# Sample tokens taken out of the dense expert stages of a PEER decoder step and served by fetched rows

## The reference, cut to what matters

```python
q = (x @ w_q).reshape(T, 8, 256)
s1, s2 = q[..., :128] @ keys1.T, q[..., 128:] @ keys2.T
v1, i1 = top_k(s1, 16);  v2, i2 = top_k(s2, 16)
sc, pos = top_k(all sums v1 + v2, 16)          # 128 experts per token
idx, gate = i1 * 128 + i2 at pos, softmax(sc)
act = gelu(einsum('tkd,td->tk', u_tab[idx], x)) * gate
out = einsum('tk,tkd->td', act, v_tab[idx])
x = x + out
```

## Time and profile before

| | us |
|---|---|
| median of 3 runs | 2356.89 (2355.27 to 2357.67) |
| profiled execution | 2357.76, span 2356.0 |
| PE busy | 2158.3 (92%) |
| DVE busy | 1722.0 (73%) |
| ACT busy | 1263.2 (54%) |
| POOL busy | 579.2 (25%) |

### The profile page before, as it was taken

The page is one execution under the profiler, slowest core; times in us unless marked ns, Lnnn a source line. Parts: engine busy times, 40 slices in busy tenths (PEclk is TensorE's granted clock), DMA queues, the critical chain, the costliest instruction groups (busy, mean ns, idle before and its releaser), DMA issues.

```text
span 2356.0 us, 53148 instructions
## 1 busy us (share of the span) xinstructions
PE 2158.3 (92%) x18562; PEld 1732.3 (74%) x18562; DVE 1722.0 (73%) x3454; ACT 1263.2 (54%) x2428; POOL 579.2 (25%) x451
## 2 busy tenths in 40 slices
PE   2477989989999999999988898998999999999998
PEld 1355867767888788888866655776788887888886
DVE  8899569966999855555544545999499996555555
ACT  2321468854444455555578454886444444555554
POOL 3996047941000000000037401786200000000000
PEclk7698799999999999999999857999999999999999
DMA  2000334545554455656554204465554545556653
GB/s 79 5 0 1 109 112 146 175 136 164 157 156 152 146 178 177 176 177 180 175 202 147 77 7 155 127 179 158 153 153 151 160 153 156 176 178 176 178 177 117
DMA packets 88953, 328.94 MB, mean 140 GB/s; under 512 B 10785, under 2 KB 10785, under 8 KB 88481
## 3 DMA queue, kind: packets, MB, share of 16 engines
q1 hardware_dynamic: 88272, 318.36, 44.7%
q0 software_dynamic: 592, 9.47, 1.0%
HBM read 321.60 MB, written 6.19 MB: 139 GB/s over the span
## 4 chain that ended last, share of the span: by engine, by line
PE 40%; issue 32%; DVE 21%; POOL 5%; ACT 1%; DVEq 0%; DMA 0%; SPq 0%; POOLq 0%; ACTq 0%
PE ps L282 11%; PE ps L284 11%; PE ps L283 11%; POOL wsp L232 2%; DVE big L800 2%; PE ps L1311 1%; DVE big L789 1%; PE ps L1867 1%; DVE big L1121 1%; DVE big L1130 1%; DVE big L1124 1%; PE ps L888 1%; DVE big L1117 1%; DVE big L1127 1%; DVE big L1149 1%
## 5 line engine op out<-in xcount | busy, mean ns | idle before, releaser
L221 ACT ACTIVATE wsp<-ring 128x512 f16<-128x512 f32 x1200 | 752.5, 629 | 802.0 <-PE ps L284 791.0
L282 PE MATMUL ps<-hs,wsp 128*128 128x288 f16 x2752 | 799.3, 290 | 48.4 <-DVE hs L307 17.6
L283 PE MATMUL ps<-hs,wsp 128*128 128x288 f16 x2752 | 799.2, 290 | 0.0
L284 PE MATMUL ps<-hs,wsp 128*128 128x288 f16 x2752 | 798.6, 290 | 0.0
L234 DVE SCALAR_TENSOR_TENSOR wsp<-ring,wsp 128x512 f16<-128x512 f32 x648 | 446.6, 692 | 406.5 <-ACT wsp L221 406.2
L283 PE MATMUL ps<-hT,wsp 128*128 128x288 f16 (+2 forms) x2560 | 641.0, 263 | 0.0
L282 PE MATMUL ps<-hT,wsp 128*128 128x288 f16 (+2 forms) x2560 | 619.7, 263 | 6.7 <-DVE hT L1451 6.7
L284 PE MATMUL ps<-hT,wsp 128*128 128x288 f16 (+2 forms) x2560 | 619.2, 263 | 0.0
L232 POOL TENSOR_TENSOR wsp<-ring,wsp 128x512 f16<-128x512 f32 x272 | 350.0, 1311 | 187.3 <-ACT wsp L221 186.5
L282 PEld LDWEIGHTS ps<-hs,wsp 128*128 128x128 f16 x2752 | 272.3, 99 | 135.7 <-DVE hs L307 25.4
L284 PEld LDWEIGHTS ps<-hs,wsp 128*128 128x128 f16 x2752 | 273.3, 99 | 73.0
(11 more groups left out here) (251 smaller groups left out, 2167.2 us busy)
## 6 DMA issues: line engine op xcount, KB each, us to landing
ring<-in_v SPq DMA_DIRECT2D x256, 512.0 KB, 3.6
ring<-in_ub SPq DMA_DIRECT2D x184, 512.0 KB, 3.7
ring<-in_ua SPq DMA_DIRECT2D x72, 512.0 KB, 3.7
ring<-in_wq SPq DMA_DIRECT2D x32, 512.0 KB, 3.6
ring<-in_win SPq DMA_DIRECT2D x32, 512.0 KB, 3.8
ring<-in_glu SPq DMA_DIRECT2D x16, 512.0 KB, 3.7
big<-in_hgs POOLq DMA_DIRECT2D x1, 4096.0 KB, 13.6
ring<-in_wout SPq DMA_DIRECT2D x8, 512.0 KB, 4.3
```

The costliest lines, as they stand in the source:

```text
L221: nc.scalar.activation(wsp[:, k % 2, 0, cols], ring[:, k, cols], ACT.Copy, scale=scale).then_inc(hi_ready, 1)
L282: nc.tensor.matmul(out, w_hi, hi, start=start, stop=False, **kw)
L283: nc.tensor.matmul(out, w_hi, lo, start=False, stop=False, **kw)
L284: return nc.tensor.matmul(out, w_lo, hi, start=False, stop=stop, **kw)
```

## The change

The 32 sample tokens leave the dense products of U and V: these have 256 columns now (`TP`), 32 groups of 8 tokens instead of 36, and no cut chunks in V (two chunks share a bank). For the samples each layer fetches the chosen rows instead. 4 copies of the 32 samples fill 128 partitions, each with 2 of the 8 heads, so 32 experts per partition (`SLOTS`). GpSimd fetches one row per partition with an indirect DMA (128 rows of 4 KB, 512 KB), 32 times from a plain copy of U and 32 times from V, into three buffers. VectorE dots each U row with the token (`dot_dve`, one per three blocks of the U loop), ScalarE takes the gelu, and VectorE sums the weighted V rows (`sum_dve`, one per 3.5 blocks of V). Eight small matmuls add the four copies up ahead of V's last four blocks.

With it the stages shift: `ua` has 28 blocks instead of 36, the transposes stand after 24 blocks instead of 40, 4 blocks of `ub` precede the loop, and the loop has 8 bodies of 12 blocks with a group after every third block. ScalarE takes the exponentials after block 20. The selection's third pass has 2 heads on 128 partitions instead of 8 on 32, and runs first; the samples' score lists shrink from 16 to 4. Three fetches stand on GpSimd's queue between its last splits and the fill. The query stage gets eight transposes that lay the samples out by rows. The loops of VectorE over U's bodies and V's blocks are unrolled.

```diff
-UA, UB = 36, 60
+UA = 28
+QH = PH // 4
+SLOTS = QH * TK
+BUFS = 3
...
-        G0 = 5
+        G0 = 1
-        TRIPS, PER = 3, 6
+        TRIPS, PER = 3, 4
-        SPOTS = [0, 2, 4, 6, 8, 10]
+        SPOTS = [0, 3, 6, 9]
+        FETCH = [2, 5, 8, 11]
...
+        def fetch_pool(g, L, a, b):
+            if a == 0:
+                g.wait_ge(pix, 2 * L + 2)
+                g.wait_ge(pxc, L + 1)
+                states_out(g, L)
+            for n in range(a, b):
+                if n >= BUFS:
+                    g.wait_ge(taken, 2 * SLOTS * L + n - BUFS + 1)
+                table, idx = (t_in[f"rows{L}"], row_u) if n < SLOTS else \
+                    (t_in[f"v{L}"].rearrange("j i d -> (j i) d"), row_v)
+                nc.gpsimd.indirect_dma_start(rows[n % BUFS], None, table, bass.IndirectOffsetOnAxis(
+                    ap=idx[:, n % SLOTS:n % SLOTS + 1], axis=0)).then_inc(fetched[n % BUFS], 16)
+        def dot_dve(v, L, n):
+            row_here(v, L, n)
+            r = rows[n % BUFS]
+            nc.vector.tensor_tensor_reduce(r, r, xrep, 1.0, 0.0, ALU.mult, ALU.add,
+                                           zs[:, n:n + 1]).then_inc(taken, 1)
+        def sum_dve(v, L, n):
+            row_here(v, L, SLOTS + n)
+            r, w = rows[(SLOTS + n) % BUFS], ws[:, n:n + 1]
+            v.wait_ge(taken, 2 * SLOTS * L + SLOTS + n)
+            if n == 0:
+                ins = nc.vector.tensor_scalar(acc, r, w, None, ALU.mult)
+            else:
+                ins = nc.vector.scalar_tensor_tensor(out=acc, in0=r, scalar=w, in1=acc, op0=ALU.mult, op1=ALU.add)
+            ins.then_inc(taken, 1)
...
                     if more:
                         weigh(d, q + 1, first)
+                    if kk in FETCH:
+                        dot_dve(v, L, d * len(FETCH) + FETCH.index(kk))
...
-            per_block(pe, f"v{L}", None, post)
+            per_block(pe, f"v{L}", None, post, 0, NK // RING - 1)
+            sample_out_pe(pe, L)
+            per_block(pe, f"v{L}", None, post, NK // RING - 1, NK // RING)
...
             split_pool(g, "ua0")
+            fetch_pool(g, 0, 0, BUFS)
             peer_ones_pool(g, 0)
+            fetch_pool(g, 0, BUFS, 2 * SLOTS)
...
-                peer_u_pe(pe, L, "ua")
-                peer_u_pe(pe, L, "ub", 0, 1)
+                peer_u_pe(pe, L, "ua", 0, 6)
                 peer_tr_pe(pe, L)
-                peer_u_pe(pe, L, "ub", 1, G0)
+                peer_u_pe(pe, L, "ua", 6, 7)
+                peer_u_pe(pe, L, "ub", 0, G0)
...
-                peer_u_act(act, L, "ua")
+                peer_u_act(act, L, "ua", 0, 5)
                 peer_exp_act(act, L)
+                peer_u_act(act, L, "ua", 5, 7)
```

More of the change, by code:

```diff
@@ L109, in build @@
         big = sb("big", [P, NK * T])
+        TAIL = NK * TP
+        xrep = big[:, TAIL:TAIL + D]
+        rows = [big[:, TAIL + D * (1 + k):TAIL + D * (2 + k)] for k in range(BUFS)]
+        sel = sb("sel", [P, TS])
         xT = sb("xT", [P, KC, T])
@@ L319, in x_chunk @@
             else:
-                eng.wait_ge(pacc[k // 2 - 1], sum(len(ACC[m]) for m in range(c + 1)))
+                eng.wait_ge(pacc[k // 2 - 1], c + 2)
         def square(c):
@@ L1031, in build, with turn_x @@
         pah = [sem(f"peer_act_hi{L}") for L in range(2)]
+        pst = sem("peer_scores_sample")
+        pxd = sem("peer_x_spread")
+        pxr = sem("peer_x_turned")
+        pxc = sem("peer_x_copied")
+        pix = sem("peer_rows_known")
+        fetched = [sem(f"peer_rows_fetched{k}") for k in range(BUFS)]
+        taken = sem("peer_rows_taken")
+        pzg = sem("peer_sample_gelu")
+        psw = sem("peer_sample_weights")
+        pso = sem("peer_sample_out")
         pal = [sem(f"peer_act_lo{L}") for L in range(2)]
         def peer_query_pe(pe, L):
+            def turn_x():
+                pe.wait_ge(pxd, L + 1)
+                for c in range(KC):
+                    mm = nc.tensor.transpose(ps[:, 2 + c // 4, (c % 4) * P:(c % 4 + 1) * P],
+                                             rows[0][:, c * P:(c + 1) * P], ident[:, :])
+                mm.then_inc(pxr, 1)
             def scores(i, k, first):
@@ L1053, in after @@
                     scores(i, k - 1, first)
-                elif not first:
+                elif first:
+                    turn_x()
+                else:
                     scores(i - 1, 3, False)
-            project(pe, f"wq{L}", lambda i, k, first: None if first else pe.wait_ge(pq[L], i * 8 + 2 * k - 6), after,
-                    inputs=(1, 4)[L])
+            for trip in range(4):
+                project(pe, f"wq{L}", lambda i, k, first: None if first else pe.wait_ge(pq[L], i * 8 + 2 * k - 6), after,
+                        trip, trip + 1, inputs=(1, 4)[L])
             scores(3, 3, False)
@@ L1086, in post @@
                     scores_out(i - 1, 3)
-            per_block(act, f"wq{L}", split_hi, post, ahead=2, following=[f"ua{L}"] * 2)
+            for trip in range(4):
+                per_block(act, f"wq{L}", split_hi, post, trip, trip + 1, ahead=2, following=[f"ua{L}"] * 2)
             scores_out(3, 3)
@@ L1114, in peer_topk_dve @@
                 v.wait_ge(pss[L], b + 1)
[L1115 to L1131, removed]
+                best([(score[:, b, j * NK:(j + 1) * NK], val[j][:, f, h], idu[j][:, f, h], rest[j][:, :])
+                      for j in range(2)])
+                if h % 4 == 3 and f:
+                    v.wait_ge(pst, 2 * L + h // 4 + 1)
+                    best([(score_s[:, h // 4, n], val[2][:, n, h // 4], idu[2][:, n, h // 4], rest[n][:, :])
+                          for n in range(2)])
         def peer_pairs_dve(v, cnt, L):
@@ L1184, in peer_pairs_dve @@
+                L_(vv.tensor_tensor(paired(ranks(past)), pos2[:, 0:n, None, :].to_broadcast(pair), paired(row(starts)),
                                     ALU.is_ge))
                 cnt.add(vv.tensor_tensor(ranks(picked[0]), ranks(past), row(steps), ALU.mult))
-                L_(vv.tensor_tensor(heads(picked[1]), heads(past), key_steps[0:w, :, None, :].to_broadcast(byhead),
+                L_(vv.tensor_tensor(heads(picked[1]), heads(past), key_steps[:, 0:nh, None, :].to_broadcast(byhead),
@@ L1405, in peer_ug_dve @@
             v.wait_ge(pge[L], GA)
-            g_bodies(v, body, 1)
+            for d in range(BODIES):
+                body(d, d == 0, d == BODIES - 1)
             v.wait_ge(pmul[L], GROUPS)
@@ L1432, in peer_v_act @@
             act.wait_ge(pge[L], NK)
+            sample_gelu_act(act, L)
             def split(act, name, i, k):
```

271 lines of the change are left out of this document (176 added, 95 removed).

## The result

| | before | after |
|---|---|---|
| median, us | 2356.08 (2355.12 to 2357.67, 4 runs) | 2298.09 (2297.08 to 2299.29, 4 runs) |
| ratio | | 0.9753, 95% interval 0.9737 to 0.9770 |
| span of the profiled execution | 2356.0 | 2297.6 |

The account below looks back on a forecast made before the run. TensorE and VectorE were both taken as full in the U loop, TensorE alone in V. Terms: -41 + 17.5 = -23.5 us per layer, -47 for two, from 2357.8 to 2311, range 2258 to 2372.

Parts of the forecast that it names:

- (a): V stage: blocks of 256 instead of 288 columns take 2.62 us instead of 2.95, minus 41 us per layer.
- the cover: V: VectorE's sums should hide behind TensorE's blocks; failing by 0.5 us per sum would cost 16 us per layer.
- a slow start: Start of V: 3 us charged for TensorE's low clock behind a long wait.
- (b): Expert selection before the U loop: a shorter VectorE chain brings TensorE's transposes at 477.5 instead of 518.6, 41 us earlier.
- (c): Transposes to U loop: GpSimd's splits, three fetches and fill precede VectorE's first split, at 512 instead of 572.35 us.
- (d): U loop: a period of 10.04 us; V starts at 834.5 instead of 817.2, plus 17.5 us per layer.
- the round: U loop: circle of VectorE's long iteration, its next split, one TensorE block and ScalarE's high part, 10.04 us per period.
- Rival 1: U loop: VectorE's own work decides, 9.4 us per period, 40 us less than forecast, 2271 us; chance 0.13.
- Rival 2: U loop: only TensorE's columns count, 8.7 us per period, 81 us less than forecast, 2230 us; chance 0.04.
- rival 4: U loop: the dot runs at the scan's rate, period 11.7 us, 102 us more than forecast, 2413; chance 0.06.
- Rival 3: GpSimd: each fetch is slow; 9 us each costs 45 us, all of the gain, 10 gives 2413; chance 0.09.
- Rival 5: U loop and V: two float32 SBUF operands halve the rate of dots and sums, 2.2 us, total 2362; chance 0.06.

Follow-up runs that it names:

- experiment 5: Changed kernel with the weighted sums of fetched v rows over 1 column instead of 1024: 2297.32 us against 2298.09.
- experiment 6: Changed kernel with the transposes behind all 28 first blocks instead of 24, and the exponentials behind 24 instead of 20: 2278.95 us against 2298.09.
- The four runs: Changed kernel with, one at a time: dots over 1 column, 2295.75 us; weighings behind the next split, 2250.40; loop products of 224 columns, 2281.93; dots done twice, 2329.46.
- experiment 2: Changed kernel with the next group's two weighings moved behind the next weight split on VectorE in the U loop: 2250.40 us against 2298.09.
- experiment 3: Changed kernel with TensorE multiplying 224 of the 256 prompt columns in the U loop: 2281.93 us against 2298.09.
- experiment 7: Changed kernel with both full-computation moves, experiment 2 and experiment 6 together: 2231.79 us against 2298.09.

## Why the prediction was right, point by point

The first reciprocal of a norm marks the stages in both traces: before 316.93, 1204.02, 1459.80 and 2347.24; after 318.71, 1175.45, 1429.66 and 2288.82. So the first layer's expert stage gained 30.4 us (23.5 forecast), the second one 28.3, the stage between them 1.6, and the start lost 1.8, which is no effect of the change (in the runs of the experiments, with the same code there, this first reciprocal stood between 316.1 and 318.9).

- **(a) V.** The block of 2.62 us is exact, the cover held (experiment 5), and the transfers came at 258 GB/s against 257, though at a share of 0.78 and not 0.85. From V's start to the next norm's reciprocal it takes 342.95 us; by the prediction, with the 5.9 us from the last product to that reciprocal before, 346. The 3 us charged for a slow start are what is missing: in the first layer TensorE begins V at the 2.4 GHz level, its products 0.11 us apart, with a wait of 3.24 us ahead of it. In the second layer, with the same wait ahead, it begins at the 1.2 GHz level (granted clock 0.50 from 1944.59 to 1947.12, products 0.21 us apart), and V takes 344.23 us, 1.3 more. So the charge was too large in both layers. In the kernel before the low clock had lasted longer (0.51 from 817.16 to 822.83); what decides is open.
- **(b) Selection.** Transposes at 479.10 instead of 477.5, of which 1.8 is the later start. That the sum fits so well is luck, as two errors cancel. The three passes begin, samples first, with these casts:

```profile
396.25 1.11 DVE L1208 CAST big<-big 128x64 f16<-128x64 uint32 x1
...
413.48 1.25 DVE L1208 CAST big<-big 128x256 f16<-128x256 uint32 x1
...
448.20 0.29 DVE L1208 CAST big<-big 128x256 f16<-128x256 uint32 x1
```

  The samples' pass took 17.2 us, 5.7 above the 11.5 taken and outside its own bounds of 8 and 15. The last pass took 28.7, to the softmax at 476.91, where a pass for 128 partitions had taken 35.6. In experiment 6, where GpSimd goes on splitting beside it, it takes 32.4; so 3.7 us of the gain in that pass come from GpSimd's pause while the exponentials are waited for, which the forecast did not have. TensorE waits ahead of the transposes in two pieces, 15.8 and 7.0 us; the forecast had some 15 in all.
- **(c) To the loop.** The chain is as told: GpSimd's splits to 489 (487 forecast), three fetches, the fill of 20.61 us (20.6), the first split at 514.20 (512). The fetches took 1.51, 0.96 and 0.94 us (1.5 each taken). Experiment 6 confirms the step by taking GpSimd's splits and fetches out of it.
- **(d) The loop.** Period 9.98 for 10.04, VectorE's idle time 0.68 for 0.6, TensorE's interval 1.05 for 1.3, the dot at 1.22 as taken, and 1.0 for the granted clock. The four runs show that the round is the cause: it takes no part of the dot, one block of three, and shrinks by order alone. The term was 4.2 us too large per layer: 1.5 from 31 periods, and 2.7 behind the last long iteration (8.6 us from there to V at 832.50, where I had 11.3). 2 of these were for the low clock behind the wait; it is there (0.50 from 514 to 520) but lies beside VectorE's first long iteration, and the first period took 9.93.
- **Rival 1** named the right next bound at the wrong place: VectorE decides once the round is loosened, at 9.20 (I had 9.4), and that is worth 48 us, by experiment 2. In the kernel as changed it doesn't decide.
- **Rival 2** falls with experiment 3, **rival 4** with the dot's 1.22 us.
- **Rival 3** needs 9 us per fetch; the groups show 0.98 and 1.12 in the mean, and the longest of the 128 took 1.86 us, though VectorE was busy nearly throughout. VectorE never waited for a row: the idle time before dots and sums is 0.0 in the groups. The Trainium skill, SBUF — State Buffer, "SBUF: two separate sides", lets a GpSimd DMA's descriptors wait for VectorE's two-port operations; no fetch here held GpSimd for longer than those 1.86 us, and whether the times from issue to landing (median 5.2 us, longest 10.1) hold such a wait is not shown.
- **Rival 5** needs 2.2 us for a dot or a sum with two float32 operands in SBUF. Measured are 1.22 and 1.28 us for 1024 elements. The Trainium skill, Vector Engine (DVE) Microarchitecture Reference, "Points that are easy to get wrong", states that the scalar-tensor-tensor form is halved by two such sources; here the measurement decides against it.

The sum of the misses is small and one-sided: 4.2 us in the loop and 3.0 in V in the first layer, 4.3 and 1.8 in the second; against them stand first splits that came 0.4 and 1.7 us late, counted from the norm's reciprocal. Of the first layer's 7.2 us, 5 were charges for a low clock at places where it wasn't granted or wasn't on the path. So the gain was 58 us and not 47.

Where did the rest of TensorE's 167 us go? In V the 0.33 us less per block shows in full. In U it doesn't. The busy time of the first layer from 391 to the loop and from there to V (columns as in the earlier trace rows, TensorE first), the changed kernel:

```profile
391.00:516.00 125.00, 93.98 (x817) 80.95 (x816) 99.17 (x260) 78.79 (x132) 91.95 (x57) 0.90 0.49 155
516.00:832.00 316.00, 281.28 (x2751) 246.73 (x2749) 291.26 (x411) 144.93 (x285) 30.74 (x32) 0.99 0.64 208
```

and the kernel before:

```profile
391.00:575.00 184.00, 172.43 (x1380) 135.37 (x1378) 144.03 (x348) 123.52 (x209) 105.76 (x68) 0.97 0.55 163
575.00:817.00 242.00, 238.81 (x2253) 196.64 (x2251) 234.08 (x318) 111.46 (x215) 0.00 (x0) 1.00 0.50 152
```

TensorE rests 31.0 + 34.7 = 66 us now and rested 11.6 + 3.2 = 15 before: 51 us more, and 52 in the second layer's same stretch (66.6 against 14.9), of the 167 - 58 = 109 in all. Three quarters of the first part are the waits of 15.8 and 7.0 us about the selection; the second is the 31 intervals of the round, 1.05 us each.

## What to carry to other kernels

Engines that are all below full and still wait for each other hint at a round that closes through a buffer slot (here one of the two of `wsp`): add up one turn of it through all engines and compare it with each engine's work per turn; if it is longer, moving work that the next engine doesn't need behind the operation it waits for is free time (48 us here, without one instruction less). New work that fits into the round's slack costs nothing, and the slack tells up to which size. And ahead of a loop that starts on several conditions, work out the second-latest one before shortening the latest: half of the fill moved away gained nothing. What the latest condition alone can give back stands in the trace as the idle time behind it: 7.42 us before the first split here.

## What the runs showed of the hardware that was not expected

- A gather of 128 rows of 4 KB keeps GpSimd only 0.98 to 1.12 us in the mean, about twice the plain DMA issue of 0.56.
- GpSimd's split slows VectorE's two-operand operations, and not its reductions. In the selection of the changed kernel the same kind of operation took 1.22 us while GpSimd waited, and 2.17 when its split began:

```profile
461.94 1.22 DVE L1251 TENSOR_TENSOR big<-big,steps 128x2048 f16<-128x2048 f16 x1
...
462.79 3.49 POOL L239 TENSOR_TENSOR wsp<-ring,wsp 128x512 f16<-128x512 f32 x2 [15.93 <-ACT wsp L228]
...
463.08 2.17 DVE L1252 TENSOR_TENSOR big<-big 128x2048 f16<-128x2048 f16 x1
...
470.28 2.18 DVE L1258 TENSOR_TENSOR big<-big,iota_h 128x2048 f16<-128x2048 f16 x1
```

In experiment 7 line 1258 took 1.22 us, with GpSimd at its fetches and not at splits:

```profile
471.67 1.22 DVE L1258 TENSOR_TENSOR big<-big,iota_h 128x2048 f16<-128x2048 f16 x1
```

The five float32 additions of experiment 6 suffered more, 4.75 us against 0.88. The reductions of this stage (L1254, L1257, L1262) took 2.27 to 2.29 us with splits beside them and without. Both engines pay: the pair of splits at 462.79 took 3.49 us, where 2.28 is its usual time.
